# Attention products of a hybrid layer with the values as the stationary operand, two heads side by side

## The reference

```python
dist = qpos[None, :, None] - sel                 # sel: the 128 keys an indexer picks
bias = bias_tab[t5_bucket(dist)]                 # 32 buckets, all distances from 128 on share one
logits = einsum('bqhd,bqkhd->bqhk', qb, k_sel) * scale + bias
logits = where(dist >= 0, logits, -inf)
p = softmax(logits, axis=-1)
return einsum('bqhk,bqkhd->bqhd', p, v_sel)
```

## Time and profile before

| | us |
|---|---|
| median of 3 runs | 695.58 (695.18 to 695.91) |
| profiled execution, its time | 696.71 |
| profiled execution, its span | 694.8 |
| PE busy in the span | 682.4 |
| DVE, ACT, POOL busy | 379.8, 260.2, 91.7 |

### The profile page before, as it was taken

One profiled execution on the slowest core, in us unless ns is written; L12 is line 12 of the kernel. 1 busy time (PEld: TensorE's weight loads), 2 busy tenths in 40 slices (PEclk: granted clock), 3 DMA queues, 4 the chain that ended last, 5 costly groups with the idle time before them and its releaser, 6 DMA issues.

```text
span 694.8 us, 8545 instructions
## 1 busy us (share of the span) xinstructions
PE 682.4 (98%) x3464; PEld 578.1 (83%) x3464; DVE 379.8 (55%) x550; ACT 260.2 (37%) x398; POOL 91.7 (13%) x130
## 2 busy tenths in 40 slices
PE   7999999999999999999999999999999999999996
PEld 5878888888988889888988888888888888888885
DVE  5766999998779778347543434244342442212215
ACT  6556334544066577226431323223232231211212
POOL 2700310000407476002000000000000000000001
PEclk9999999999999999999999999999999999999999
DMA  9443032432521303160431232332423323233203
GB/s 264 127 148 117 8 120 83 133 119 61 183 62 60 122 1 117 52 196 0 152 122 55 67 122 68 115 110 72 122 66 116 110 72 122 66 116 106 76 1 121
DMA packets 49352, 68.59 MB, mean 99 GB/s; under 512 B 5025, under 2 KB 39841, under 8 KB 49314
## 3 DMA queue, kind: packets, MB, share of 16 engines
q1 hardware_dynamic: 45744, 60.16, 27.1%
q0 software_dynamic: 3280, 7.35, 3.0%
q10 hardware_dynamic: 290, 0.55, 0.2%
HBM read 65.40 MB, written 4.74 MB: 101 GB/s over the span
## 4 chain that ended last, share of the span: by engine, by line
PE 91%; DVE 3%; ACT 2%; issue 1%; DMA 1%; POOL 0%; SPq 0%; DVEq 0%; POOLq 0%
PE PS L1139 79%; PE PS L1330 2%; PE PS L1213 2%; PE PS L1188 1%; PE PS L1189 1%; PE PS L1341 1%; PE PS L1250 1%; DMA A<-in_x_dram 1%; PE PS L1237 1%; ACT A L700 1%; DVE w_lo L785 1%; PE PS L1183 1%; PE PS L1223 1%; ACT A L717 0%; DVE A L1071 0%
## 5 line engine op out<-in xcount | busy, mean ns | idle before, releaser
L1139 PE MATMUL PS<-hT_lo,w_hi 128*128 128x512 f32 (+2 forms) x584 | 218.7, 374 | 0.9 <-DVE hT_lo L789 0.6
L1139 PE MATMUL PS<-hT_hi,w_lo 128*128 128x512 f32 (+2 forms) x584 | 217.2, 372 | 0.0
L1139 PE MATMUL PS<-hT_hi,w_hi 128*128 128x512 f32 (+2 forms) x584 | 217.2, 372 | 0.0
L785 DVE TENSOR_TENSOR w_lo<-raw,w_hi 128x2048 fp32r<-128x2048 f32 x50 | 116.7, 2334 | 179.8 <-ACT w_hi L547 179.6
L547 ACT ACTIVATE w_hi<-raw 128x2048 fp32r<-128x2048 f32 x50 | 95.7, 1914 | 212.9 <-PE PS L1139 212.3
L1139 PEld LDWEIGHTS PS<-hT_lo,w_hi 128*128 128x128 f32 (+1 forms) x584 | 109.7, 188 | 20.0 <-issue 1.0
L1139 PEld LDWEIGHTS PS<-hT_hi,w_hi 128*128 128x128 f32 (+1 forms) x584 | 109.6, 188 | 19.7
L1139 PEld LDWEIGHTS PS<-hT_hi,w_lo 128*128 128x128 f32 (+1 forms) x584 | 109.7, 188 | 18.4
L1139 PE MATMUL PS<-w_hi,ff 128*128 128x512 f32 x352 | 108.4, 389 | 0.0
L1139 PEld LDWEIGHTS PS<-w_hi,ff 128*128 128x128 f32 x352 | 66.1, 188 | 13.6
L1139 PE MATMUL PS<-w_lo,ff 128*128 128x512 f32 x176 | 68.5, 389 | 0.0
(11 more groups left out here) (168 smaller groups left out, 751.4 us busy)
## 6 DMA issues: line engine op xcount, KB each, us to landing
raw<-in_w_in_dram SPq DMA_DIRECT2D x16, 1024.0 KB, 5.7
raw<-in_w_gate_dram SPq DMA_DIRECT2D x11, 1024.0 KB, 5.2
raw<-in_w_up_dram SPq DMA_DIRECT2D x11, 1024.0 KB, 5.3
raw<-in_w_down_dram SPq DMA_DIRECT2D x11, 1024.0 KB, 4.9
raw<-in_w_o_dram SPq DMA_DIRECT2D x4, 1024.0 KB, 4.9
A<-in_x_dram SPq DMA_DIRECT2D x4, 512.0 KB, 5.7
A<-in_x_dram POOLq DMA_DIRECT2D x4, 512.0 KB, 4.9
out_dram<-A SPq DMA_DIRECT2D x8, 256.0 KB, 2.0
```

The source lines that it names most:

```text
L785: dve.tensor_tensor(lo, raw_view(j), hi.bitcast(F32), ALU.subtract).then_inc(s_lo, 1)
L1139: o = pe.matmul(out, lhs[a], rhs[b], start=(first and n == 0), stop=(last and n == 2))
```

## The change

Five edits. (1) In the product of probabilities and values the values are stationary (64 columns) and the transposed probabilities move (128 columns); two heads of a block are done together, on output partitions 0 to 63 and 64 to 127, at every second step; `PT` has four buffers. The result is transposed already. (2) So the reciprocals of the row sums are widened on DVE, brought into the transposed form by PE (a float32 matmul with the identity), copied to SBUF by ACT and multiplied in by DVE; the transposes of y go. (3) The unit order is changed, heads 6 and 7 of blocks 0 and 1 come as pairs. (4) The output splits of the recurrence move to steps 10, 13, 16 and 19 (19 is the last of four, 2 later on DVE). (5) POOL subtracts the far bias from the table at the start, so that far keys need no bias: `BM` gets a bias in the nearest 256 keys alone, and the mask for the others is copied for the first three units of a late block.

```diff
-    unit_order = [(0, h) for h in range(HEADS_B - 2)] + [(1, h) for h in range(5)] + [(0, HEADS_B - 2), (0, HEADS_B - 1)]
-    unit_order += [(1, h) for h in range(5, HEADS_B)] + [(b, h) for b in range(2, TB) for h in range(HEADS_B)]
+    unit_order = [(b, h) for b in (0, 1) for h in range(HEADS_B - 2)]
+    unit_order += [(b, h) for b in (0, 1) for h in (HEADS_B - 2, HEADS_B - 1)] + [(b, h) for b in range(2, TB) for h in range(HEADS_B)]
-    Y_A_AT = {23 + 2 * h: h for h in range(HEADS_A)}
+    Y_A_AT = {10 + 3 * h: h for h in range(HEADS_A)}
...
+        def ends_before(i, lag):
+            if not 0 <= i - lag < UNITS:
+                return None
+            b, h = unit_order[i - lag]
+            return b if h == HEADS_B - 1 else None
...
-            if u >= 2:
-                eng.wait_ge(s_pv, u - 1)
-            copy(PT[u % 2][:, 0:n], PS[:, 2 + u % 2, 0:n]).then_inc(s_pts[u % 2], 1)
+            if u >= 4:
+                eng.wait_ge(s_pv, (u - 4) // 2 + 1)
+            copy(PT[u % 4][:, 0:n], PS[:, 2 + u % 2, 0:n]).then_inc(s_pts[u % 2], 1)
...
+            pool.wait_ge(s_small, 64)
+            pool.wait_ge(s_far, 16)
+            pool.tensor_tensor(tab, tab, far[0:N_BUCKETS, :], ALU.subtract).then_inc(s_tab, 1)
...
-            pool.wait_ge(s_far, 16)
-            pool.tensor_copy(Bh[:, :, 0:S - NEAR], far[:, :].unsqueeze(2).to_broadcast([P, HEADS_B, S - NEAR])
-                             ).then_inc(s_bfar, 1)
...
-                pool.tensor_tensor(BM[u % 3][:, 0:n], M, Bh[:, h, (TB - 1 - b) * P:S], ALU.subtract).then_inc(s_bm, 1)
+                beyond = max(n - NEAR, 0)
+                if beyond and unit_order[u - 3][0] != b:
+                    pool.tensor_copy(BM[u % 3][:, 0:beyond], M[:, 0:beyond])
+                pool.tensor_tensor(BM[u % 3][:, beyond:n], M[:, beyond:n], Bh[:, h, S - (n - beyond):S],
+                                   ALU.subtract).then_inc(s_bm, 1)
...
+            def take_sums(b):
+                act.wait_ge(s_rps, b + 1)
+                if b >= 2:
+                    act.wait_ge(s_ylo, b - 1)
+                act.activation(y_sb[b % 2], PS[:, 6, :], ACT.Copy).then_inc(s_rsb, 1)
...
-                b = block_done(i - 4)
+                b = ends_before(i, 4)
+                if b is not None:
+                    take_sums(b)
+                b = block_done(i - 2)
                 if b is not None:
                     y_hi_b(b)
...
+            def widen_sums(b):
+                dve.wait_ge(s_ex, ended(b))
+                if b:
+                    dve.wait_ge(s_rps, b)
+                link(dve.reciprocal(rs[:, :], sm[:, 8 * b:8 * b + 8]))
+                dve.tensor_copy(r_wide.rearrange("p (h d) -> p h d", d=DH),
+                                rs[:, :].unsqueeze(2).to_broadcast([P, HEADS_B, DH])).then_inc(s_rw, 1)
...
+                dve.wait_ge(s_rsb, b + 1)
+                dve.wait_ge(s_pv, ended(b) // 2)
+                dve.tensor_tensor(y_sb[b % 2], PS[:, 4 + b % 2, :], y_sb[b % 2], ALU.mult).then_inc(s_yb, 1)
...
+                b = ends_before(i, 2)
+                if b is not None:
+                    widen_sums(b)
                 b = block_done(i - 1)
                 if b is not None:
                     y_norm_b(b)
-                b = block_done(i - 5)
+                b = block_done(i - 4)
...
+            pe.wait_ge(s_tab, 1)
             pe.matmul(PS[0:HEADS_B, 6, :], tab, oh_sb[:, 0:S], start=True, stop=True)
...
-            def turn_y_b(b):
-                pe.wait_ge(s_yb, b + 1)
-                if b >= 1:
-                    pe.wait_ge(s_ylo, b)
+            def spread_sums(b):
+                pe.wait_ge(s_rw, b + 1)
+                if b:
+                    pe.wait_ge(s_rsb, b)
                 for k in range(4):
-                    o = pe.transpose(PS[:, 6, k * P:(k + 1) * P], yb[b % 2][:, k * P:(k + 1) * P], ident[:, :])
-                o.then_inc(s_ybt, 1)
+                    o = pe.matmul(PS[:, 6, k * P:(k + 1) * P], r_wide[:, k * P:(k + 1) * P], ident[:, :],
+                                  start=True, stop=True)
+                o.then_inc(s_rps, 1)
...
-                if i >= PV_LAG:
+                if i >= PV_LAG and (i - PV_LAG) % 2:
                     u = i - PV_LAG
-                    b, h = unit_order[u]
-                    pe.wait_ge(s_pts[u % 2], u // 2 + 1)
+                    b, h = unit_order[u - 1]
+                    for e in range(2):
+                        pe.wait_ge(s_pts[e], u // 2 + 1)
...
                     for s in range(b + 1):
-                        o = pe.matmul(PS[:, 4 + b % 2, h * DH:(h + 1) * DH], PT[u % 2][:, s * P:(s + 1) * P],
-                                      av[:, s * W + h * DH:s * W + (h + 1) * DH], start=(s == 0), stop=(s == b))
+                        for e in range(2):
+                            o = pe.matmul(PS[e * DH:(e + 1) * DH, 4 + b % 2, h // 2 * P:(h // 2 + 1) * P],
+                                          av[:, s * W + (h + e) * DH:s * W + (h + e + 1) * DH],
+                                          PT[(u - 1 + e) % 4][:, s * P:(s + 1) * P], start=(s == 0), stop=(s == b))
                     o.then_inc(s_pv, 1)
...
-                b = block_done(i - 3)
+                b = ends_before(i, 4)
                 if b is not None:
-                    turn_y_b(b)
+                    spread_sums(b)
...
-                        turn_y_b(TB - 1)
+                        pe.wait_ge(s_yb, TB)
```

More of the change, by code:

```diff
@@ L110, in hymba_layer @@
         w_lo = sb("w_lo", [P, 2, CH], F32R)
-        N1, N2 = FT * 2 * S, 7936
+        N1, N2 = FT * 2 * S, 8448
         low = ExitStack()
@@ L140, in hymba_layer @@
         sm = sb("sm", [P, UNITS])
-        rs = sb("rs", [P, UNITS])
+        rs = sb("rs", [P, HEADS_B])
         def a1(o, n):
@@ L163, in hymba_layer @@
         Pb = [a1(19456 + 512 * i, 512) for i in range(4)]
-        PT = [a1(21504 + 512 * i, 512) for i in range(2)]
-        yb = [a1(2048, 512), a1(2560, 512)]
+        PT = [a1(21504, 512), a1(22016, 512), a1(2560, 512), a1(3584, 512)]
+        y_sb = [a1(2048, 512), A2[:, 7936:8448]]
         scr = [a1(6144 + 1024 * i, 1024) for i in range(TB)]
@@ L182, in hymba_layer @@
         raw_ikw = A2[:, 7296:7296 + KT * IKW]
+        r_wide = A2[:, 7296:7808]
         Bh = A2[:, 0:4096].rearrange("p (h c) -> p h c", h=HEADS_B)
@@ L222, in hymba_layer @@
         s_bh = sem("bias_tile_landed")
-        s_bfar = sem("far_bias_spread")
+        s_tab = sem("table_from_far_bias")
         s_sth = sem("stack_hi_ready")
@@ L257, in hymba_layer @@
         s_pv = sem("pv_done")
-        s_yb = sem("attention_y_normed")
-        s_ybt = sem("attention_yT_psum")
+        s_rw = sem("reciprocal_sums_widened")
+        s_rps = sem("reciprocal_sums_psum")
+        s_rsb = sem("reciprocal_sums_sbuf")
+        s_yb = sem("attention_yT_normed")
         s_yha = sem("recurrent_yT_hi_ready")
@@ L370, in slot_free @@
             elif w_slot(j) == 2:
-                eng.wait_ge(s_pv, UNITS)
+                eng.wait_ge(s_pv, UNITS // 2)
         def w_split(j):
@@ L515, in _ @@
             pool.wait_ge(s_bh, 16 * HEADS_B)
-            pool.wait_ge(s_bfar, 1)
             for u in range(UNITS):
@@ L643, in y_hi_a @@
                 act.activation(hT_hi[:, h, :], hb(gT, h), ACT.Copy).then_inc(s_yha, 1)
+            def take_sums(b):
[3 more added lines that the diff above has]
+                act.activation(y_sb[b % 2], PS[:, 6, :], ACT.Copy).then_inc(s_rsb, 1)
             def y_hi_b(b):
-                act.wait_ge(s_ybt, b + 1)
+                act.wait_ge(s_yb, b + 1)
                 act.activation(hT_hi[:, 4:8, b * P:(b + 1) * P],
-                               PS[:, 6, :].rearrange("p (k t) -> p k t", t=P), ACT.Copy).then_inc(s_yhi, 1)
+                               y_sb[b % 2].rearrange("p (k t) -> p k t", t=P), ACT.Copy).then_inc(s_yhi, 1)
             def attend(i):
@@ L958, in y_lo_b @@
                 dve.wait_ge(s_yhi, b + 1)
-                dve.tensor_tensor(hT_lo[:, 4:8, b * P:(b + 1) * P],
-                                  PS[:, 6, :].rearrange("p (k t) -> p k t", t=P),
+                dve.tensor_tensor(hT_lo[:, 4:8, b * P:(b + 1) * P], y_sb[b % 2].rearrange("p (k t) -> p k t", t=P),
                                   hT_hi[:, 4:8, b * P:(b + 1) * P].bitcast(F32), ALU.subtract).then_inc(s_ylo, 1)
-            def y_norm_b(b):
[L964 to L972, removed]
+            def widen_sums(b):
[5 more added lines that the diff above has]
+                                rs[:, :].unsqueeze(2).to_broadcast([P, HEADS_B, DH])).then_inc(s_rw, 1)
+            def y_norm_b(b):
+                dve.wait_ge(s_rsb, b + 1)
+                dve.wait_ge(s_pv, ended(b) // 2)
+                dve.tensor_tensor(y_sb[b % 2], PS[:, 4 + b % 2, :], y_sb[b % 2], ALU.mult).then_inc(s_yb, 1)
             def attend(i):
@@ L1319, in attend @@
                     stacked_dots(PS[:, qk_bank(i), 0:(b + 1) * P], b, h, h).then_inc(s_qk, 1)
```

(9 more changed lines are left out.)

## The result

The changed kernel takes 697.0 us (median of 12 runs, 696.2 to 697.59) against 695.24 us for the kernel before beside it: a ratio of 1.0023, 95% interval 1.0015 to 1.0030. It is slower by about 1.8 us where 4.2 us of gain were forecast.

What follows compares the result with a forecast made beforehand. TensorE, busy 98% of the span, was taken as the bound. The terms summed to -4.4 us, rounded to -4.2; from the profiled 696.71 us, less 1.13 to the median, this gave 691.4 us, range 689.2 to 696.3 us.

Steps and rivals of the forecast that it cites:

- Products: Probabilities times values in the attention loop: the two heads' halves overlap, 0.111 us for a pair of records, 7.9 us saved.
- C: Rival on the products: half an overlap, 0.16 us for a pair of records, 695.3 us, no change; chance 0.10.
- D: Rival on the products: no overlap, the two halves follow each other, 699.3 us, slower; chance 0.09.
- E: Rival on the products: weight loads not hidden, 0.213 us for a pair of records, 698.5 us; chance 0.05.
- Changes of shape: PE switching into and out of the 16 half-wide pair blocks: 0.09 us a side, 2.9 us added, bounds 0 and 5.1.
- Normalisation: Transposes of y go, float32 matmuls spreading the reciprocal sums come in on PE: net 2.1 us added.
- The low clock: PE's low clock at 248 to 251.4 us, behind the stop, was expected not to recur: 1.6 us saved.
- Splits of the recurrence: ACT copies and DVE subtractions move to units 10 to 21, where DVE is nearly full: 1.0 us added, bounds 0 and 2.5.
- The order and the stop: PE's stop at 244.95 to 246.40 us shortens from 1.45 to about 0.9 us by the new unit order: 0.5 us saved.
- Short waits: PE's short waits on y, expected to go with the transposes of y: 0.4 us saved.
- Bias for near keys: POOL's add shrinks to 256 columns, giving room under the last block's shorter step; in itself it saves nothing.
- rival B: DVE and ACT bound units 10 to 23, 1.5 us more than set for the waits: 692.9 us; chance 0.12.

Runs made afterwards that it cites:

- a3: The changed kernel with all key blocks of the even head first, then all of the odd head: 699.43 us, ratio 1.0054 to the kernel before.
- a1: The changed kernel with the output splits of the recurrence back at steps 23, 25, 27 and 29: 694.50 us, ratio 0.9984 to the kernel before.
- b1: The kernel before with only the splits of the recurrence moved to steps 10, 13, 16 and 19: 697.63 us, ratio 1.0030.
- b4: The kernel before with only the new unit order: 695.95 us, ratio 1.0005.
- b3: The kernel before with only the bias for near keys and the table subtracted at the start: 695.43 us, ratio 0.9999.
- a6: The changed kernel with the splits late and POOL's add over all keys again: 696.28 us, ratio 1.0012 to the kernel before.

## Why the prediction was wrong

By its own steps, with the size set and the size found:

- **Products, -7.9 us: right.** 16, 12, 8 and 4 records take 1.02, 0.81, 0.59 and 0.37 us (PE timeline after); the slope is 0.65/12 = 0.054 us a record, as set (0.108 us for a pair against 0.111). Rivals C, D and E fall, and a3 shows the mechanism.
- **Changes of shape, +2.9 us: too small.** The same four sizes leave 0.155 us beside the slope in each block, and in front of a block 0.10 us: 272.48 - 272.15 = 0.33 us against 0.23 us for the 512 columns of the logits. The transposes behind a block take 0.05 us more as well: four of them 273.92 - 273.50 = 0.42 us, against 0.37 us in the earlier trace rows; one, two and three show the same. That is 0.30 us for each of 16 blocks, 4.9 us, where 2.9 us were set (its upper bound was 5.1). The row I used for the way back mixed it with another transition and I took 0.09 for both.
- **Normalisation, +2.1 us: right as PE work.** The four spreadings take 0.91, 0.88, 0.81 and 1.04 us, 3.6 in all. On PE the change therefore saves about 7.9 - 4.9 - 2.1 = 0.9 us of work, not 2.9. The traces agree: without the listed waits the loop is 34.3 us long in a1 and 35.0 us in the second trace of the kernel before.
- **The low clock, -1.6 us: this step failed.** I read it as a consequence of the stop that every execution has. It was in the profiled execution and in 2 of 77 later ones. I had written down that this execution lay 1.13 us above the median and subtracted the difference at the end, and in the same sum took a gain for the very thing that made the difference, counting it twice.
- **Splits of the recurrence, +1.0 us: the step that decides.** 2.5 us in the changed kernel (a1), 2.0 us in the kernel before (b1). This step failed by its size. The reason was named (DVE full where they go), but the price was put at less than half. I relied on a float of two to three steps; DVE's list is in order, and one block of 2.2 us in it uses the float up at once. The stretching of DVE's SBUF-only instructions beside POOL, some 0.9 us of these 2.2, was not in the sum.
- **The order and the stop, -0.5 us: not there.** The order alone brings no gain (b4), and in the changed kernel the stop ends later, not earlier. I looked for what ended the stop and not for what is late next: the transposes of unit 8.
- **Short waits, -0.4 us:** not found; what PE no longer waits for y, it waits for copies and exponentials.
- **Bias for near keys, 0 by itself and needed with the rest: right**, by b3 and a6. **The start: hidden: right**, b3.

The differences are 2.0 + 1.6 + 1.5 + 0.5 + 0.4 = 6.0 us, against 697.0 - 691.4 = 5.6 us, or 5.8 us without the rounding of -4.4 to -4.2. This closes better than its parts are known, as the terms of waits overlap (b1's 2.0 or a1's 2.5 can stand for the splits). The price of rival B was right: 1.0 us and 1.5 more is the 2.5 us of a1. Its time, 692.9 us, was 4 us too low because it kept the other wrong terms, the clock above all. The upper end of the range was also added up too low: C with the upper bound of the waits is 695.3 + 1.5 = 696.8 us, not 696.3. The sign of the result hung on one moved line: the rest of the change is worth 1.1 us (a1), and the early splits cost 2.0 to 2.5.

Where a1's 1.1 us lie can be read from the traces. In the loop PE has 0.7 us less to do and 0.4 us more of listed waits (1.7 against 1.3). Behind it, the output product up to the first transpose of the next stage takes 38.2 us instead of 38.7, in every trace with the change against every trace without it, most of it by the last transposes of y (0.36 us), which are gone. That is 0.8 us of the 1.1. What stays open is what each of a1's waits on ACT's copies is due to, and what the new order is worth in the changed kernel.

## What to carry to other kernels

Take a term of a sum only from what several executions share: a low clock in a trace whose own time lies above the other runs is not the kernel's, and crediting its removal counts the same microsecond twice. When the bound engine's work shrinks, go through the next engine's list in order, instruction by instruction, around the place where something is added; its busy share over 10 us says that it is near its limit, not how much one block of 2 us in it will cost. And price each edit of a bundle by itself: here one line, the place of four splits, hid a version that is 0.2% faster than the kernel before, or 0.3% with the transposes for the reciprocals.

## What the runs showed of the hardware

Two float32 matmuls with 64 stationary columns each, on output partitions 0 to 63 and 64 to 127, run at the same time: 0.108 us for a pair of records of 128 moving columns when the two heads alternate. With up to four records of a half in a row nothing is lost (8 records take 0.59 to 0.60 us in both orders); with more, each further record costs 0.11 us instead of 0.054 (a3: 16 records take 1.51 us instead of 1.02). The weight loads of the halves (136 ns against 198 in the earlier trace rows) are hidden:

```profile
L1359 PEld LDWEIGHTS PS<-A 128*64 128x64 f32 x160 | 8.5, 136 | 3.6 <-issue 2.8
```

A pair of records would need about 0.107 us of loading (the prediction's estimate of 0.053 us a load) and 0.107 us of streaming, and it takes 0.108 us. So a load runs beside a matmul that uses the same rows of the array. A switch between the full-wide and the half-wide form costs about 0.10 us going in, and coming out up to 0.155 us and another 0.05 us on the transposes that follow: 0.30 us for a round trip.

A DVE instruction with two SBUF inputs and a POOL instruction on SBUF hold each other up. DVE's split of 128x512 takes 0.68 to 0.69 us in every trace when POOL is idle, and 1.15 us when it starts 0.13 us behind an add of POOL; a 128x128 copy of POOL that starts during the split takes 0.75 us against 0.28. Which of the two waits depends on who starts first. A pair of traces shows that POOL is the cause: b3 changes nothing in this stage but POOL's work, and the same split, at the same time of the kernel, falls from 0.92 to 0.69 us (second trace of the kernel before, then b3 with the POOL add that starts behind it):

```profile
266.19 0.92 DVE L955 TENSOR_TENSOR hT_lo<-A,hT_hi 128x512 fp32r<-128x512 f32 x1
...
266.20 0.69 DVE L958 TENSOR_TENSOR hT_lo<-A,hT_hi 128x512 fp32r<-128x512 f32 x1
266.36 1.11 POOL L529 TENSOR_TENSOR A<-A 128x256 f32<-128x256 f32 x1 [0.34 <-DVE nm L984]
```

There POOL pays: its add takes 1.11 us, and 0.74 us alone. DVE's widening copy, 128x512 within SBUF, takes 0.97 us beside POOL and 0.43 us when POOL is idle:

```profile
278.19 0.43 DVE L988 COPY A<-rs 128x512 f32<-128x512 f32 x1
```

The Trainium skill (SBUF — State Buffer, SBUF: two separate sides) says that DVE and GpSimd take turns on a shared pair of ports, as an exclusive lock, for DVE instructions with two SBUF inputs or in a two-port mode. These rows agree: where both starts can be read, the one that starts second is the longer one.
